# Rotary queries regrouped: latent-query, latent-key and rotation steps of a two-block transformer forward pass

## What is computed

```python
q = (rmsnorm(c_q, q_norm_g) @ w_uq).reshape(B, S, 8, 96)     # 384 -> 8 x (64 + 32)
q_nope = q[..., :64]
q_rope = apply_rope(q[..., 64:], cos, sin)                   # the last 32 of each head
k_rope = apply_rope(k_r, cos, sin)                           # one, shared by all heads
ckv = rmsnorm(c_kv, kv_norm_g)
k_nope = (ckv @ w_uk).reshape(B, S, 8, 64)                   # 256 -> 8 x 64
v = (ckv @ w_uv).reshape(B, S, 8, 64)
# apply_rope: t1, t2 = halves of 16; [t1*cos - t2*sin, t2*cos + t1*sin]
```

## Time and profile before

| what | value |
|---|---|
| median of 3 runs | 2862.82 us (2862.77 to 2864.18) |
| span of the profiled execution | 2861.2 us |
| TensorE busy | 2805.8 us, 98% of the span |
| VectorE busy | 1842.9 us, 64% |
| ScalarE busy | 1299.2 us, 45% |
| mean granted TensorE clock | 0.996 |

### The profile page before, as it was taken

The page is one execution under the profiler, slowest core; times in us unless marked ns, Lnnn a source line. Parts: engine busy times, 40 slices in busy tenths (PEclk is TensorE's granted clock), DMA queues, the critical chain, the costliest instruction groups (busy, mean ns, idle before and its releaser), DMA issues.

```text
span 2861.2 us, 51128 instructions
## 1 busy us (share of the span) xinstructions
PE 2805.8 (98%) x21992; PEld 2669.5 (93%) x21992; DVE 1842.9 (64%) x3008; ACT 1299.2 (45%) x1860; POOL 71.9 (3%) x66
## 2 busy tenths in 40 slices
PE   8999999999999999999999999999999999999998
PEld 8999799999999889999999888799999998888998
DVE  5668576665666766766666557666666654666665
ACT  5445444444444545444444334444464433544443
POOL 0000000000000010000000001100000000110000
PEclk9999999999999999999999999999999999999999
DMA  7554366555555445555565653355555566435553
GB/s 257 180 166 130 111 173 203 177 183 186 189 168 169 112 149 177 176 179 179 192 208 160 187 145 116 96 178 191 177 175 180 168 195 141 133 89 166 180 184 108
DMA packets 481282, 474.52 MB, mean 166 GB/s; under 512 B 47105, under 2 KB 464417, under 8 KB 480929
## 3 DMA queue, kind: packets, MB, share of 16 engines
q1 hardware_dynamic: 477472, 460.75, 51.5%
q0 software_dynamic: 3584, 10.49, 1.4%
HBM read 464.91 MB, written 6.29 MB: 165 GB/s over the span
## 4 chain that ended last, share of the span: by engine, by line
PE 90%; DVE 5%; ACT 3%; DMA 1%; issue 1%; SPq 0%; DVEq 0%; ACTq 0%
PE ps L945 33%; PE ps L1044 33%; PE ps L1065 16%; PE ps L1182 2%; PE ps L1106 2%; DVE WL L1875 1%; PE ps L1151 1%; ACT WH L1496 1%; PE ps L992 1%; PE ps L996 1%; PE ps L988 1%; DMA RAW<-in_w_in 0%; PE ps L976 0%; DMA RAW<-in_w_branch 0%; DVE REGION L2030 0%
## 5 line engine op out<-in xcount | busy, mean ns | idle before, releaser
L1875 DVE TENSOR_TENSOR WL<-RAW,WH 128x2048 fp32r<-128x2048 f32 (+2 forms) x390 | 871.5, 2240 | 414.6 <-ACT WH L1496 412.6
L1496 ACT ACTIVATE WH<-RAW 128x2048 fp32r<-128x2048 f32 (+2 forms) x398 | 736.8, 1864 | 162.3 <-DMA RAW<-in_w_in 83.9
L1065 PE MATMUL ps<-HL,WH 128*128 128x256 f32 x1408 | 394.0, 280 | 0.0
L1065 PE MATMUL ps<-HH,WH 128*128 128x256 f32 x1408 | 393.6, 280 | 0.0
L1065 PE MATMUL ps<-HH,WL 128*128 128x256 f32 x1408 | 393.0, 279 | 0.0
L945 PE MATMUL ps<-UH,WH 128*128 128x256 f32 x1328 | 382.6, 288 | 3.4 <-DVE WL L1875 3.4
L1044 PE MATMUL ps<-UH,WH 128*128 128x256 f32 x2688 | 374.8, 282 | 0.5 <-DVE WL L1875 0.5
L945 PE MATMUL ps<-UL,WH 128*128 128x256 f32 x1328 | 374.5, 282 | 0.0
L945 PE MATMUL ps<-UH,WL 128*128 128x256 f32 x1328 | 374.3, 282 | 0.0
L1044 PE MATMUL ps<-UL,WH 128*128 128x256 f32 x2688 | 373.4, 281 | 0.0
L1044 PE MATMUL ps<-UH,WL 128*128 128x256 f32 x2688 | 373.3, 281 | 0.0
(11 more groups left out here) (326 smaller groups left out, 3710.0 us busy)
## 6 DMA issues: line engine op xcount, KB each, us to landing
RAW<-in_w_ffn_in SPq DMA_DIRECT2D x88, 1024.0 KB, 5.1
RAW<-in_ffn_wi SPq DMA_DIRECT2D x88, 1024.0 KB, 5.1
RAW<-in_w_in SPq DMA_DIRECT2D x86, 1024.0 KB, 5.5
RAW<-in_w_ffn_out SPq DMA_DIRECT2D x32, 1024.0 KB, 4.9
RAW<-in_ffn_wo SPq DMA_DIRECT2D x32, 1024.0 KB, 5.0
RAW<-in_w_out SPq DMA_DIRECT2D x16, 1024.0 KB, 5.0
RAW<-in_w_ffn_out SPq DMA_DIRECT2D x16, 768.0 KB, 4.2
RAW<-in_ffn_wo SPq DMA_DIRECT2D x16, 768.0 KB, 4.2
```

What stands on the lines that cost most here:

```text
L1065: last = nc.tensor.matmul(bank(n + side, 0, T), a[:, k, side * P:(side + 1) * P], b[:, k0 + k, :], start=k0 + k == 0 and a is wh and b is ...
L1496: nc.scalar.activation(split_ap(s, part_high(s)), raw_ap(s), ACT.Copy).then_inc(weights_high, 1)
L1875: v_.tensor_tensor(split_ap(s, part_low(s)), raw_ap(s), split_ap(s, part_high(s)).bitcast(FP), ALU.subtract)\
```

## The change

The columns of w_uq are put into another order on the host, once: for each four heads their 4 x 64 plain features and then their 4 x 32 rotary features. So uq becomes 6 products of 128 features: two heads' plain rows to a product, and one product with the rotary rows of four heads on all 128 partitions (tile QR). uk makes two heads to a product, 4 products of 128. ScalarE takes a product of two heads apart with two copies of 64 rows. VectorE swaps the halves of QR's groups of 32 partitions with one shuffle for all heads, multiplies on 128 partitions, and writes the sums to QH by 8 adds, one for each head. The four 32 x 512 swap products go; the one for the shared key stays. The tables of sine and cosine are made on 128 partitions, with the sign in the sines, instead of on 32. QR and TURNED take 2 x 512 words of room that the recurrence's HK no longer needs by then.

```diff
-        pl.slabs(L + "uq", [4, 4], places=MIX)
+        pl.slabs(L + "uq", [3, 3], places=MIX)
-        pl.slabs(L + "uk", [8], places=MIX)
+        pl.slabs(L + "uk", [4], places=MIX)
-        pl.products(L + "swap", 5)
+        pl.products(L + "swap", 1)
...
-                sp.dma_start(COS[64:96, :].bitcast(I32), w["pos"]).then_inc(inputs_in, 16)
+                sp.dma_start(COS[:].bitcast(I32), w["pos"]).then_inc(inputs_in, 16)
...
-                    for m in range(4):
-                        n = first[L + "uq"] + 4 * i + m
-                        product(n, [(bank(n)[0:QK, 0:T], [(slot(s, 3, 384)[:, k, m * QK:(m + 1) * QK], CQ[:, k, :]) for k in range(3)])])
+                    for m in range(3):
+                        n = first[L + "uq"] + 3 * i + m
+                        product(n, [(bank(n, 0, T), [(slot(s, 3, 384)[:, k, m * P:(m + 1) * P], CQ[:, k, :]) for k in range(3)])])
...
-                for m in range(MLA_H):
+                for m in range(MLA_H // 2):
                     n = first[L + "uk"] + m
-                    product(n, [(bank(n)[0:NOPE, 0:T], [(slot(s, 2, 512)[:, k, m * NOPE:(m + 1) * NOPE], CKV[:, k, :]) for k in range(2)])])
+                    product(n, [(bank(n, 0, T), [(slot(s, 2, 512)[:, k, m * P:(m + 1) * P], CKV[:, k, :]) for k in range(2)])])
...
-                swap = con("swap", ROPE, slice(64, 96))
-                for h in range(MLA_H):
-                    wait_evicted(pe, first[L + "uq"] + h)
-                for m in range(4):
-                    n = first[L + "swap"] + m
-                    product(n, [(bank(n)[64:96, :], [(swap, QH[64:96, 2 * m:2 * m + 2, :])])])
-                n = first[L + "swap"] + 4
-                product(n, [(bank(n)[64:96, 0:T], [(swap, KR[64:96, 0, :])])])
+                wait_evicted(pe, first[L + "win7"])
+                n = first[L + "swap"]
+                product(n, [(bank(n)[64:96, 0:T], [(con("swap", ROPE, slice(64, 96)), KR[64:96, 0, :])])])
...
-                for h in range(MLA_H):
-                    evict(first[L + "uq"] + h, QH[0:QK, h, :], bank(first[L + "uq"] + h)[0:QK, 0:T])
-                for h in range(MLA_H):
-                    evict(first[L + "uk"] + h, KH[0:NOPE, h, :], bank(first[L + "uk"] + h)[0:NOPE, 0:T])
+                def head_pair(n, dst, h):
+
+                    wait_product(act, n)
+                    nc.scalar.activation(dst[0:NOPE, h, :], bank(n)[0:NOPE, 0:T], ACT.Copy)
+                    nc.scalar.activation(dst[0:NOPE, h + 1, :], bank(n)[NOPE:P, 0:T], ACT.Copy).then_inc(evicted[n % BANKS], 1)
+
+                for i in range(2):
+                    n = first[L + "uq"] + 3 * i
+                    head_pair(n, QH, 4 * i)
+                    head_pair(n + 1, QH, 4 * i + 2)
+                    evict(n + 2, QR[:, i, :], bank(n + 2, 0, T))
+                for m in range(MLA_H // 2):
+                    head_pair(first[L + "uk"] + m, KH, 2 * m)
...
-                for m in range(4):
-                    if m == 2:
-                        for i in range(2):
-                            wait_evicted(dve, first[L + "hg.o"] + i)
-                        v_.tensor_tensor(HG_SQ, OT, OT, ALU.mult).then_inc(squares_ready, 1)
-                        feed.to(slab_first[L + "hg.gate0"] + 1)
-                    n = first[L + "swap"] + m
-                    q = QH[64:96, 2 * m:2 * m + 2, :]
-                    turned = TMP[64:96, m % 2, :].rearrange("p (g t) -> p g t", g=2)
-                    wait_product(dve, n)
-                    v_.tensor_tensor(turned, bank(n)[64:96, :].rearrange("p (g t) -> p g t", g=2), sin2, ALU.mult)\
-                      .then_inc(evicted[n % BANKS], 1)
-                    wait_evicted(dve, n)
-                    link(v_.tensor_tensor(q, q, cos2, ALU.mult))
-                    link(v_.tensor_tensor(q, q, turned, ALU.add))
-                n = first[L + "swap"] + 4
+                cos2, sin2 = (a[:].unsqueeze(1).broadcast_to([P, 2, T]) for a in (COS, SIN))
+                for i in range(2):
+                    wait_evicted(dve, first[L + "uq"] + 3 * i + 2)
+                half = ROPE // 2
+                link(v_.stream_shuffle(TURNED, QR, [(i + half) % ROPE for i in range(ROPE)]))
+                link(v_.tensor_tensor(TURNED, TURNED, sin2, ALU.mult))
+                link(v_.tensor_tensor(QR, QR, cos2, ALU.mult))
+                for i in range(2):
+                    wait_evicted(dve, first[L + "hg.o"] + i)
+                v_.tensor_tensor(HG_SQ, OT, OT, ALU.mult).then_inc(squares_ready, 1)
+                feed.to(slab_first[L + "hg.gate0"] + 1)
+                for h in range(MLA_H):
+                    q = slice(h % 4 * ROPE, (h % 4 + 1) * ROPE)
+                    v_.tensor_tensor(QH[64:96, h, :], QR[q, h // 4, :], TURNED[q, h // 4, :], ALU.add)
+                n = first[L + "swap"]
```

More of the change, by code:

```diff
@@ L120, in constants @@
     for i in range(ROPE // 2):
-        swap[64 + ROPE // 2 + i, i] = -1.0
+        swap[64 + ROPE // 2 + i, i] = 1.0
         swap[64 + i, ROPE // 2 + i] = 1.0
@@ L125, in constants @@
     inv = (np.float32(10000.0) ** (-np.arange(0, ROPE, 2, dtype=np.float32) / np.float32(ROPE))).astype(np.float32)
-    freq[64:96, 0] = np.concatenate([inv, inv])
+    freq[:, 0] = np.tile(np.concatenate([-inv, inv]), P // ROPE)
     put("freq", freq)
@@ L541, in build @@
         Z, HK = region(HG_H * T), region(HG_H * T)
+        QR, TURNED = (HK[:, i * 2 * T:(i + 1) * 2 * T].rearrange("p (g t) -> p g t", t=T) for i in range(2))
         used[0] = both
@@ L1282, in _ @@
                 pe.wait_ge(roped, l + 1)
-                for m in range(MLA_H):
+                for m in (0, 1, 3, 4):
+                    wait_evicted(pe, first[L + "uq"] + m)
+                for m in range(MLA_H // 2):
                     wait_evicted(pe, first[L + "uk"] + m)
@@ L1614, in tables @@
                     act.wait_ge(angle_ready, 1)
-                    nc.scalar.activation(SIN[64:96, :], SIN[64:96, :], ACT.Sin)
-                    nc.scalar.activation(COS[64:96, :], COS[64:96, :], ACT.Sin).then_inc(rope_ready, 1)
+                    nc.scalar.activation(SIN[:], SIN[:], ACT.Sin)
+                    nc.scalar.activation(COS[:], COS[:], ACT.Sin).then_inc(rope_ready, 1)
                 if q == 2:
@@ L2133, in tables @@
                     dve.wait_ge(inputs_in, 32)
-                    link(v_.tensor_copy(V[64:96, :], COS[64:96, :].bitcast(I32)))
-                    link(v_.tensor_scalar(V[64:96, :], V[64:96, :], con("freq", 1, slice(64, 96)), None, ALU.mult))
+                    link(v_.tensor_copy(V[:], COS[:].bitcast(I32)))
+                    link(v_.tensor_scalar(V[:], V[:], con("freq", 1), None, ALU.mult))
                 if q < 2:
                     table, turn = ((SIN, 0.0), (COS, 0.25))[q]
-                    a, n, r = V[64:96, :], TMP[64:96, 0, T:2 * T], table[64:96, :]
+                    a, n, r = V[:], TMP[:, 0, T:2 * T], table[:]
                     link(v_.tensor_scalar(n, a, 1.0 / (2.0 * np.pi), turn, ALU.mult, ALU.add))
@@ L2567 @@
     arrays = {name: np.ascontiguousarray(inputs[name]) for name in _WEIGHTS}
+    uq = arrays["w_uq"].reshape(DEPTH, Q_LORA, 2, MLA_H // 2, QK)
+    parts = [uq[..., a:b].reshape(DEPTH, Q_LORA, 2, -1) for a, b in ((0, NOPE), (NOPE, QK))]
+    arrays["w_uq"] = np.ascontiguousarray(np.concatenate(parts, axis=-1).reshape(DEPTH, Q_LORA, -1))
     arrays["cst"] = constants()[0]
@@ L2572 @@
     arrays["pT"] = np.ascontiguousarray(np.asarray(inputs["p_2"])[:, 0].transpose(0, 2, 1))
-    arrays["pos"] = np.ascontiguousarray(np.broadcast_to(np.asarray(inputs["positions"]), (ROPE, T)))
+    arrays["pos"] = np.ascontiguousarray(np.broadcast_to(np.asarray(inputs["positions"]), (P, T)))
     nc = _bacc.Bacc("TRN2", target_bir_lowering=False, num_devices=1)
```

2 lines of the change are left out of this document (removed).

## The result

The changed kernel took 2841.35 us (median of 4 runs, 2839.04 to 2843.35) beside 2862.89 for the kernel before on the same chip (4 runs): ratio on record 0.9931, 95% interval 0.9917 to 0.9945 (the two medians by themselves give 0.9925). By the medians it is faster by 21.5 us; forecast were 25.8. In a second series of runs it had 2838.78 (5 runs, 2838.24 to 2841.02) beside 2860.05 (9 runs), ratio 0.9925 (0.9913 to 0.9938).

The account below looks back on a forecast made before the run. TensorE, with 90% of the chain, was taken as the bound. Layer 0's 13.7 and layer 1's 12.1 made 25.8 us off 2861.2, 2835.4; with 1.6 for the median of the runs, 2837.0, range 2834.0 to 2842.2.

Parts of the forecast that it names:

- uq, uk: Query and key products on TensorE: 36 and 16 fewer matmul records, 2.67 and 3.60 us off in each layer.
- 96 or 64 output features make no difference: In uq and uk, a matmul record takes 0.2175 or 0.220 us; with 128 features 0.2159.
- swap, hg.o: Swap: one 256-column product stays, 4.30 and 3.67 us off; hg.o: at the full clock, 2.43 and 1.42 off.
- the clock falls all the same: Rival: swap products didn't lower the clock, hg.o stays at 1.2 GHz; 4.9 us less gained, 2841.9; chance 0.11.
- Shuffle: VectorE's shuffle before hg.o's eviction ends: taken as 0.69 us, at most 2.30; up to 1.3 costs nothing.
- gate0 to gate1: VectorE's adds, 2.8 to 3.5 us, shared key and WL end at S + 12.7 to 13.4, before TensorE's S + 13.5.
- so the 0.73 and 0.72 waits go: TensorE's waits at gate1's first matmul for VectorE's WL vanish: 0.73 us in layer 0, 0.72 in layer 1.
- a new wait takes part of it: Rival: first gate0 slab, ScalarE's evictions, shuffle or held adds late; one to two us a layer, 2839 to 2841; chance 0.16.
- A few tenths of contention fit into that: Loads around gate0: SyncE's next loads come 4 to 6 us earlier beside the memory tokens' load; WL keeps 1.4 us cover.
- the sum: All terms added: 13.7 us off in layer 0, 12.1 in layer 1, together 25.8 off the profiled execution's 2861.2.
- Everything behind gate1 is started by product numbers and moves along: Work after gate1 in the kernel: shifts earlier with the change, no term of its own in the forecast.

Follow-up runs that it names:

- lower group: Kernel before, no edit: the 38 of 80 executions that lie at 2857.8 to 2861.0 us, median 2858.9.
- upper group: Kernel before, no edit: the 42 of 80 executions that lie at 2862.1 to 2868.3 us, median 2863.6.
- the second execution: The changed kernel profiled once more with nothing edited: 2838.78 us, profiled span 2838.5.
- pauses filled: Changed kernel with unused 128 x 128 matmuls in front of four waits of TensorE: 2836.49 us, 2836.79 in later runs.
- filled form: Kernel before with the same unused matmuls in front of the same four waits of TensorE: 2862.27 us (12 runs).

## Why the prediction was off

The 2841.35 lie 4.3 us above the forecast and 0.85 inside the upper end of its range. The ratio on record, 0.9931, would make it 2843 from 2862.8, just outside.

**uq, uk:** right as sizes. uq stands in 7.87 us (7.77 forecast), uk in 3.46. The reason given for uk ("96 or 64 output features make no difference") holds only for outputs in the same half of the partitions.

**swap, hg.o:** the mechanism was right and the rival "the clock falls all the same" wrong: 1.00 and 2.64 us in both profiles of the changed kernel. But the terms "4.30 off", "3.67 off", "2.43 and 1.42 off" are those of executions in which the clock falls. Where it doesn't, swap is 3.98 - 0.54 = 3.44 and hg.o nothing. The change takes away a toss-up. With the median of all nine unedited runs of the changed kernel, 2840.25, it gains 18.7 us against the lower group and 23.4 against the upper; with 2838.8, the five of the second series, 20.1 and 24.8.

**Shuffle:** 0.74 for the 0.69 taken (the estimate of 0.8 beside it is mis-scaled: by width, a quarter, it would be 0.6), and hidden: the squares behind the two multiplies still waited 0.25 us for hg.o's eviction.

**gate0 to gate1:** "so the 0.73 and 0.72 waits go" was too much in the profiled execution: 0.42 and 0.54 stayed. VectorE's adds took the 3.5 forecast as the upper value; the WL of the second gate0 slab ended 5.6 us behind gate0's start and not 5.1, since ScalarE waited 0.46 for its load. That is the rival "a new wait takes part of it", by another road than forecast, the transfers in place of the shuffle or the evictions. "A few tenths of contention fit into that" was the judgement that failed: the slabs took 7.3 us and not 5.5. In the second execution layer 0 had no wait for the slab and no bracket; in layer 1 the slab made WH 2.19 late and cost TensorE 1.40.

**The step that failed is the sum.** It took 25.8 from one execution and held the clock fixed everywhere else ("Everything behind gate1 is started by product numbers and moves along"). The change's own stretches gave 24.9 in the profiled pair; 5.3 were lost again outside them, 4.4 of these at pauses of TensorE that the change doesn't touch and behind which the clock falls in some executions. That a single profile is one draw of such falls was missing, both for the kernel before (the swap stretch) and for the changed one. The 24.9 are luck too, since the kernel before was drawn from its upper group; against the lower one the same stretches would give about 20. With the pauses filled, the changed kernel measured 2836.5. That this is near the forecast of 2837.0 does not confirm it, since filling also takes away falls that the kernel before has.

## What to carry to other kernels

Before pricing a stretch at a lowered clock, look at several executions: two groups of times that the mean clock of a run tells apart (mostly 0.997 and 0.995 to 0.996 here) are a sign that the fall is a toss-up, and its price counts by its share. Here matmuls of 64 output features cost half when they alternated between the two halves of the output partitions, so merging them would have gained nothing there. And when TensorE's work ahead of a stretch shrinks, the loads are next: look at which transfer can be moved out of it.

## What the runs showed of the hardware

- TensorE's clock fell while it was busy without a gap, with 32 x 32 matmuls of 512 columns. With 4 of them a layer it did in one profile of the kernel before and in that of its filled form, not in the other profile; by the two groups of times that is 42 of 80 executions. With 8 added, it did in both layers of the profile, and all ten runs were above 2858.8, where the full clock would have given 2852 by the estimate made before.
- Behind pauses of 1.5 to 2.8 us it fell in some executions and not in others; three such differences cost 1.3, 1.5 and 1.6 us.
- Two matmuls of 64 features into different halves of the partitions started 0.01 to 0.06 us apart: 0.114 us each in place of 0.22.
- A shuffle within groups of 32 partitions took 0.74 us for 128 x 512 and 0.44 for 32 x 256, a multiply of the same shape 0.69 and 0.42.
